# Layer 0's attention: values multiplied four items behind the scores, maps joined by one operation, negated maxima, squares of two blocks at once

## The reference, cut to what matters

```
def _diff_attend(q, k, v, lam):
    s = jnp.einsum('bqhmd,bkhmd->bhmqk', q, k).astype(jnp.float32) / math.sqrt(q.shape[-1])
    p = jax.nn.softmax(s, axis=-1)
    a = p[:, :, 0] - lam * p[:, :, 1]
    return jnp.einsum('bhqk,bkhd->bqhd', a.astype(v.dtype), v)

def out_proj(o):                       # inside _diff_mixer
    o = _rmsnorm(o, subln_g) * (1.0 - lam_init)
    return o.reshape(o.shape[0], o.shape[1], -1) @ w_o
```

## Time and profile before

| | |
|---|---|
| median of 3 runs | 3017.91 us (3016.14 to 3020.22) |
| the profiled execution | 3016.83 us, of which the span of instructions is 3015.6 us |
| TensorE busy over the span | 2670.6 us (89%) |
| vector engine busy | 751.3 us (25%) |
| scalar engine busy | 483.6 us (16%) |
| DMA | 690.23 MB, mean 229 GB/s |

### The profile page before, as it was taken

How to read it: one execution, slowest core, us unless ns; L and a number is a source line. 1 busy time by engine, 2 the same in 40 slices (tenths; PEclk the granted TensorE clock), 3 DMA queues, 4 the chain that set the end, 5 groups by cost and what they waited for, 6 DMA issues and landing times.

```text
span 3015.6 us, 57462 instructions
## 1 busy us (share of the span) xinstructions
PE 2670.6 (89%) x24534; PEld 1982.5 (66%) x24534; DVE 751.3 (25%) x2039; ACT 483.6 (16%) x1182; POOL 212.8 (7%) x392
## 2 busy tenths in 40 slices
PE   8999999999999999997998899988776998776676
PEld 7888788887888778885444456665555466544444
DVE  2002520023002430014116621211113163332323
ACT  2001310011001220003104521110002151000001
POOL 1001010011001010001000012221211000000000
PEclk9999999999999999998999999999988999999999
DMA  7553465546453455542320039999996314999997
GB/s 265 179 171 112 157 239 173 174 157 223 153 192 111 162 202 203 195 157 106 144 84 29 3 144 375 411 411 421 420 420 236 105 52 179 420 419 419 419 419 296
DMA packets 251832, 690.23 MB, mean 229 GB/s; under 512 B 15247, under 2 KB 142942, under 8 KB 235230
## 3 DMA queue, kind: packets, MB, share of 16 engines
q1 hardware_dynamic: 240352, 675.27, 59.0%
q0 software_dynamic: 7552, 10.76, 1.0%
q10 hardware_dynamic: 3710, 0.99, 0.1%
HBM read 669.95 MB, written 17.04 MB: 228 GB/s over the span
## 4 chain that ended last, share of the span: by engine, by line
PE 76%; DMA 12%; DVE 5%; issue 3%; ACT 3%; SPq 0%; ACTq 0%; POOL 0%; POOLq 0%; DVEq 0%
PE ps L663 18%; DMA arena<-in_moe_w_up 11%; PE ps L674 10%; PE ps L1443 5%; PE ps L2287 5%; PE ps L2262 3%; PE ps L2790 3%; PE ps L2302 3%; PE ps L1497 2%; PE ps L894 2%; PE ps L687 2%; PE ps L1054 2%; PE ps L2042 2%; PE ps L2751 1%; PE ps L2814 1%
## 5 line engine op out<-in xcount | busy, mean ns | idle before, releaser
L663 PE MATMUL ps<-arena 128*128 128x256 f32 x2560 | 568.6, 379 | 3.5 <-DVE arena L745 3.5
L663 PEld LDWEIGHTS ps<-arena 128*128 128x128 f32 x2560 | 483.0, 189 | 73.8 <-issue 4.1
L674 PE MATMUL ps<-arena 128*128 128x256 f32 x1408 | 318.0, 379 | 0.0
L674 PEld LDWEIGHTS ps<-arena 128*128 128x128 f32 x1408 | 264.9, 189 | 46.1 <-issue 8.4
L2287 PE MATMUL ps<-arena 128*32 128x128 f32 x6016 | 193.6, 286 | 61.1 <-issue 58.6
L2287 PEld LDWEIGHTS ps<-arena 128*32 128x32 f32 x6016 | 177.6, 115 | 71.9 <-issue 67.6
L2790 PE MATMUL ps<-arena 128*32 128x128 f32 x4096 | 138.7, 294 | 82.3 <-issue 80.6
L787 DVE TENSOR_TENSOR arena<-arena,ps 128x256 f32<-128x256 f32 x76 | 32.1, 422 | 638.4 <-ACT arena L755 633.7
L2790 PEld LDWEIGHTS ps<-arena 128*32 128x32 f32 x4096 | 125.5, 118 | 90.0 <-issue 89.0
L1443 PE MATMUL ps<-arena 128*128 128x512 f32 (+1 forms) x384 | 162.6, 601 | 5.6 <-ACT arena L1390 5.6
L755 ACT ACTIVATE arena<-ps 128x256 f32<-128x256 f32 x76 | 29.2, 384 | 675.1 <-PE ps L663 675.1
(11 more groups left out here) (457 smaller groups left out, 3091.6 us busy)
## 6 DMA issues: line engine op xcount, KB each, us to landing
arena<-in_moe_w_gate SPq DMA_DIRECT2D x64, 2048.0 KB, 24.8
arena<-in_moe_w_up SPq DMA_DIRECT2D x64, 2048.0 KB, 25.5
arena<-in_moe_w_down SPq DMA_DIRECT2D x64, 2048.0 KB, 30.4
arena<-in_mod_w SPq DMA_DIRECT2D x24, 2048.0 KB, 13.0
arena<-in_w_gate SPq DMA_DIRECT2D x44, 1024.0 KB, 5.3
arena<-in_w_up SPq DMA_DIRECT2D x44, 1024.0 KB, 7.9
arena<-in_w_down SPq DMA_DIRECT2D x44, 1024.0 KB, 4.8
arena<-in_w_in SPq DMA_DIRECT2D x12, 1024.0 KB, 6.0
```

What stands on the lines that cost most here:

```text
L663: last = pe.matmul(k.ps[:, T % 4, off:off + S], w[:, t, T % 2 * P:(T % 2 + 1) * P], h[:, t, :], start=(t == 0), stop=(t == KT - 1), skip_g ...
L674: last = pe.matmul(acc[:, t, :], d[:, T % 2, t * P:(t + 1) * P], k.hid[:, T % 4, :], start=(T == 0 and t % 2 == 0), stop=end, skip_group_c ...
```

## The change

In layer 0's attention:

- The factor 0.125 moves from the exponentials and the negation into the queries, where they are projected. For that the projection's two products become three-operand operations with a constant factor (0.125 for q0, 1 for all other tags), and the context's copy gets a scale.
- The maximum is written negated; the operation of line 1599 is gone.
- The maps are joined unnormalised by the first sum: with the row sums s0 and s1, p0 + (-lam s0 / s1) p1 is made by one operation over the map, with a one-element operation ahead of it for the factor. The operation over the whole second map (line 1607) is gone. The missing 1/s0 comes in when the output is copied out of PSUM.
- The values' matmuls, and with them the output's copy, run four items behind the scores.
- The squares are taken for two blocks at once, every second item, five items behind, without an accumulated sum; the vector engine sums them, six items behind. The root waits for the last of these sums.
- The small statistics lie in six rows of ten columns in place of four of sixteen.

Cut to its core:

```diff
+def factor_of(tag):
+    return 0.125 if tag == "q0" else 1.0
...
 def dve_project_tile(k, tag, dst, ntok, j):
-    V.tensor_tensor(dst[:, j, 0:S], k.ps[:, j % 4, 0:S], k.c["cosx"], ALU.mult).then_inc(*s["pr_cos"].up(tag, j))
+    V.scalar_tensor_tensor(dst[:, j, 0:S], k.ps[:, j % 4, 0:S], f, k.c["cosx"], ALU.mult, ALU.mult).then_inc(*s["pr_cos"].up(tag, j))
     V.wait_ge(*s["pr_rot"].at(tag, j))
-    V.tensor_tensor(tmp, k.ps[:, 4 + j % 2, 0:S], k.c["sinx"], ALU.mult).then_inc(*s["pr_sin"].up(tag, j))
+    V.scalar_tensor_tensor(tmp, k.ps[:, 4 + j % 2, 0:S], f, k.c["sinx"], ALU.mult, ALU.mult).then_inc(*s["pr_sin"].up(tag, j))
...
 def pe_attend(k, l, items):
-    N, maps = len(items), 2 if l else 1
-    for n in range(N + 3):
+    N, maps, behind = len(items), 2 if l else 1, 3 if l else 4
+    for n in range(N + behind):
...
-        i = n - 3
+        i = n - behind
...
 def dve_attend_a(k, items):
-            V.tensor_reduce(st[:, 0:2], ps[:, 2 * (n % 2):2 * (n % 2) + 2, 0:nk], AX, ALU.max).then_inc(*step.up())
-            V.wait_ge(*step.last())
-            V.tensor_scalar(st[:, 2:4], st[:, 0:2], -0.125, None, ALU.mult).then_inc(*step.up(0, n))
+            V.tensor_reduce(stats(k, n)[:, 0:2], ps[:, 2 * (n % 2):2 * (n % 2) + 2, 0:nk], AX, ALU.max, negate=True).then_inc(*step.up(0, n))
...
             V.reciprocal(st[:, 6:8], st[:, 4:6]).then_inc(*step.up())
             V.wait_ge(*step.last())
-            V.tensor_scalar(pr[:, 1, :], pr[:, 1, :], st[:, 7:8], k.lam[:, 2:3], ALU.mult, ALU.mult).then_inc(*step.up())
+            V.scalar_tensor_tensor(st[:, 8:9], st[:, 4:5], k.lam[:, 2:3], st[:, 7:8], ALU.mult, ALU.mult).then_inc(*step.up())
             V.wait_ge(*step.last())
-            V.scalar_tensor_tensor(pr[:, 0, :], pr[:, 0, :], st[:, 6:7], pr[:, 1, :], ALU.mult, ALU.add).then_inc(*s["wt_dve"].up(0, i))
-        i = n - 3
-        if i >= 0:
+            V.scalar_tensor_tensor(pr[:, 0, :], pr[:, 1, :], st[:, 8:9], pr[:, 0, :], ALU.mult, ALU.add).then_inc(*s["wt_dve"].up(0, i))
+        i = n - 4
+        if 0 <= i < N:
             q, t = items[i][0], items[i][1]
             V.wait_ge(*s["av_done"].at(0, i))
-            V.tensor_copy(rows_of(k)[:, t, q * P:(q + 1) * P], ps[:, 6 + i % 2, 0:P]).then_inc(*s["av_out_dve"].up(0, i))
+            V.tensor_scalar(rows_of(k)[:, t, q * P:(q + 1) * P], ps[:, 6 + i % 2, 0:P], stats(k, i)[:, 6:7], None, ALU.mult).then_inc(*s["av_out_dve"].up(0, i))
+        i = n - 6
+        if i >= 0 and i % 2:
+            q, t = items[i][0], items[i][1]
+            V.wait_ge(*s["av_squared"].at(0, i))
+            V.tensor_reduce(k.ss.rearrange("p (t h) -> p t h", t=4)[:, t - 1:t + 1, q:q + 1], two_blocks(k.rscale2), AX, ALU.add).then_inc(*s["av_summed"].up(0, i))
...
 def act_attend_a(k, items):
-                last = act.activation(pr[:, m, :], ps[:, 2 * (n % 2) + m, 0:nk], ACT.Exp, bias=st[:, 2 + m:3 + m], scale=0.125, accum_out=st[:, 4 + m:5 + m])
+                last = act.activation(pr[:, m, :], ps[:, 2 * (n % 2) + m, 0:nk], ACT.Exp, bias=st[:, m:1 + m], accum_out=st[:, 4 + m:5 + m])
             last.then_inc(*s["sc_exp"].up(0, n))
-        i = n - 4
-        if i >= 0:
+        i = n - 5
+        if i >= 0 and i % 2:
             q, t = items[i][0], items[i][1]
             act.wait_ge(*s["av_out_dve"].at(0, i))
-            if i > 0:
-                act.wait_ge(*s["av_squared"].at(0, i - 1))
-            act.activation(k.rscale2[:, 0:P], rows_of(k)[:, t, q * P:(q + 1) * P], ACT.Square,
-                           accum_out=k.ss[:, t * 8 + q:t * 8 + q + 1]).then_inc(*s["av_squared"].up(0, i))
+            if i >= 2:
+                act.wait_ge(*s["av_summed"].at(0, i - 2))
+            act.activation(two_blocks(k.rscale2), rows_of(k)[:, t - 1:t + 1, q * P:(q + 1) * P], ACT.Square).then_inc(*s["av_squared"].up(0, i))
...
 def act_attention_a_end(k):
-    act.wait_ge(*s["av_squared"].last())
+    act.wait_ge(*s["av_summed"].at(0, len(items_a()) - 1))
```

More of the change, by code:

```diff
@@ L1464, in act_project_tile @@
     if ntok > S:
[L1465 removed]
+        act.activation(dst[:, j, S:2 * S], k.ps[:, j % 4, S:2 * S], ACT.Copy, scale=factor_of(tag)).then_inc(*s["pr_copied"].up(tag, j, "ctx"))
 def dve_project(k, tag, dst, ntok, tiles):
@@ L1473, in dve_project_tile @@
 def dve_project_tile(k, tag, dst, ntok, j):
-    V, s = k.nc.vector, k.s
+    V, s, f = k.nc.vector, k.s, factor_of(tag)
     tmp = k.pr2[:, j % 2, 0:S]
     V.wait_ge(*(s["pr_copied"].at(tag, j, "ctx") if ntok > S else s["pr_copied"].at(tag, j)))
-    V.tensor_tensor(dst[:, j, 0:S], k.ps[:, j % 4, 0:S], k.c["cosx"], ALU.mult).then_inc(*s["pr_cos"].up(tag, j))
+    V.scalar_tensor_tensor(dst[:, j, 0:S], k.ps[:, j % 4, 0:S], f, k.c["cosx"], ALU.mult, ALU.mult).then_inc(*s["pr_cos"].up(tag, j))
     V.wait_ge(*s["pr_rot"].at(tag, j))
-    V.tensor_tensor(tmp, k.ps[:, 4 + j % 2, 0:S], k.c["sinx"], ALU.mult).then_inc(*s["pr_sin"].up(tag, j))
+    V.scalar_tensor_tensor(tmp, k.ps[:, 4 + j % 2, 0:S], f, k.c["sinx"], ALU.mult, ALU.mult).then_inc(*s["pr_sin"].up(tag, j))
     V.wait_ge(*s["pr_cos"].last())
@@ L1591, in dve_attend_a @@
     step = s["sc_dve"]
-    for n in range(N + 3):
+    for n in range(N + 6):
         if n < N:
             nk = items[n][4]
-            st = k.st[:, n % 4, :]
             V.wait_ge(*s["sc_done"].at(0, n))
-            V.tensor_reduce(st[:, 0:2], ps[:, 2 * (n % 2):2 * (n % 2) + 2, 0:nk], AX, ALU.max).then_inc(*step.up())
-            V.wait_ge(*step.last())
-            V.tensor_scalar(st[:, 2:4], st[:, 0:2], -0.125, None, ALU.mult).then_inc(*step.up(0, n))
+            V.tensor_reduce(stats(k, n)[:, 0:2], ps[:, 2 * (n % 2):2 * (n % 2) + 2, 0:nk], AX, ALU.max, negate=True).then_inc(*step.up(0, n))
         i = n - 1
@@ L1602, in dve_attend_a @@
             nk = items[i][4]
-            pr, st = probs(k, i, nk), k.st[:, i % 4, :]
+            pr, st = probs(k, i, nk), stats(k, i)
             V.wait_ge(*s["sc_exp"].at(0, i))
@@ L1606, in dve_attend_a, with stats, two_blocks @@
             V.wait_ge(*step.last())
-            V.tensor_scalar(pr[:, 1, :], pr[:, 1, :], st[:, 7:8], k.lam[:, 2:3], ALU.mult, ALU.mult).then_inc(*step.up())
+            V.scalar_tensor_tensor(st[:, 8:9], st[:, 4:5], k.lam[:, 2:3], st[:, 7:8], ALU.mult, ALU.mult).then_inc(*step.up())
             V.wait_ge(*step.last())
-            V.scalar_tensor_tensor(pr[:, 0, :], pr[:, 0, :], st[:, 6:7], pr[:, 1, :], ALU.mult, ALU.add).then_inc(*s["wt_dve"].up(0, i))
-        i = n - 3
-        if i >= 0:
+            V.scalar_tensor_tensor(pr[:, 0, :], pr[:, 1, :], st[:, 8:9], pr[:, 0, :], ALU.mult, ALU.add).then_inc(*s["wt_dve"].up(0, i))
+        i = n - 4
+        if 0 <= i < N:
             q, t = items[i][0], items[i][1]
             V.wait_ge(*s["av_done"].at(0, i))
-            V.tensor_copy(rows_of(k)[:, t, q * P:(q + 1) * P], ps[:, 6 + i % 2, 0:P]).then_inc(*s["av_out_dve"].up(0, i))
+            V.tensor_scalar(rows_of(k)[:, t, q * P:(q + 1) * P], ps[:, 6 + i % 2, 0:P], stats(k, i)[:, 6:7], None, ALU.mult).then_inc(*s["av_out_dve"].up(0, i))
[4 more added lines that the diff above has]
+            V.tensor_reduce(k.ss.rearrange("p (t h) -> p t h", t=4)[:, t - 1:t + 1, q:q + 1], two_blocks(k.rscale2), AX, ALU.add).then_inc(*s["av_summed"].up(0, i))
+def stats(k, n):
+    return k.st.rearrange("p a b -> p (a b)")[:, n % 6 * 10:n % 6 * 10 + 10]
+def two_blocks(tile):
+    return tile.rearrange("p (t d) -> p t d", t=2)
 def act_attend_a(k, items):
@@ L1619, in act_attend_a @@
     N = len(items)
-    for n in range(N + 4):
+    for n in range(N + 5):
         if n < N:
             nk = items[n][4]
-            st, pr = k.st[:, n % 4, :], probs(k, n, nk)
+            st, pr = stats(k, n), probs(k, n, nk)
             act.wait_ge(*s["sc_dve"].at(0, n))
```

2 lines of the change are left out of this document (1 added, 1 removed).

## The result

The changed kernel takes 2999.21 us in the median (2992.55 to 3001.21), the kernel before beside it 3017.86; the ratio is 0.9934, with a 95% interval of 0.9917 to 0.9951. That is 18.65 us faster, inside the range of 2990 to 3009 and 3 us above the 2996 forecast. The profiled execution took 3001.21 us (span 3000.0), 15.6 us less span than the one before.

The account below looks back on a forecast made before the run. Layer 0's attention was held half by the vector engine, half by a copy-values-transposes-scores loop. Gains of 3.0, 16.5 and 4.3 us made 23.8, less 1.8 for small delays 22.0: 2996 us, range 2990 to 3009.

Parts of the forecast that it names:

- the loop: Layer 0's attention, half of each head: copy of the turned map, values, transposes and next scores hold the pace, 5.44 us.
- The loop over three items: Layer 0's attention with later values: the copy-values-transposes-scores chain takes 5.08 us against 5.92 of vector work; TensorE next, 8.14 a head.
- The fear about 0.03 us of margin: Layer 0's attention: some scores arrive only about 0.03 us early, so small delays add 0.2 us a head, 1.8 us.
- The vector engine's head, 8.64: Layer 0's attention: vector operations of one head of four items, summed by start distances, cost 8.64 us, above TensorE's 8.14.
- the deduction: 1.8 us taken off the 23.8 us gain for small delays of scores in layer 0's attention, leaving 22.0.
- first head: Start of layer 0's attention: falls from 11.60 to 8.64 us, taken as a full head, gain 3.0 us.
- six heads: Middle of layer 0's attention: 68.32 us less six heads at 8.64, gain 16.5 us.
- last stretch: End of layer 0's attention, to the reciprocal behind the root: 18.41 us becomes 14.06, gain 4.3 us.
- The last sum is hidden under the table load: End of layer 0's attention: the root's table load starts behind the square without awaiting the sum; otherwise 0.45 us.
- The gain passes one for one: Behind layer 0's attention: the expert weight stream's start moves with the stage, so the stage's gain reaches the kernel's end.
- rival (c): Layer 0's attention: TensorE, nearly full, meets its low clock; at share 0.6 13 us slower, 3031 us; chance 0.04.
- The Trainium skill's rule: Layer 0's attention: no two vector operations overlap, so a head takes 9.6 us, 8 us more in all, 3004; chance 0.06.

Follow-up runs that it names:

- the lag alone: Kernel before with only the values' matmuls, their copy out and the squares one item later, operations unchanged: stage 86.32 us, head 10.03, median 11.5 us faster.
- the cuts alone: Changed kernel with values' matmuls back to three items behind, squares and sums one item earlier: stage 89.24 us, head 10.45.

## Why the prediction was right

- *What bounds the stage.* Right on both counts: the loop (the lag alone removes the wait) and the vector engine (the cuts alone keep the wait of 0.91). The expectation for the lag alone, 10.05 us a head out of rows 2, met 10.03.
- *The loop over three items stops binding, TensorE is next.* Right: 1.8 us of waits left in the middle stretch, and once the vector engine was relieved it was TensorE that worked throughout (34.00 of 34.00 us, at 8.48 a head). The square's new wait and the copy's wait in the same iteration cost nothing there. The fear about 0.03 us of margin, for which I took off 1.8 us (0.2 us a head would be 1.6 over eight), didn't come true: no gap in the vector engine's rows.
- *The vector engine's head, 8.64.* It measured 9.08. Two terms were too small. The one-element factor, priced by the negation's 0.17, took 0.219, and the scaled copy out, priced by the plain copy's 0.29, took 0.345. That is 0.05 and 0.06 per item, 0.11 x 4 = 0.44 a head, exactly the difference. The others of the vector engine were right: the sum 0.411 (0.43 taken), the negated maximum 1.217 against 1.222, so free. The paired square of the scalar engine was sized wrong, 0.413 for 0.32, but that engine had room. The projections' products with three operands, taken as 0.05 dearer each, cost nothing: 0.419 and 0.423 against 0.420 and 0.424.
- *The sum.* 23.8 us before the deduction, 22.0 forecast, 20.7 measured. By parts, against the forecast ahead of the deduction: first head 3.1 (3.0), six heads 14.0 (16.5), last stretch 3.6 (4.3), together 20.7. The 2.5 us of the six heads are the two prices; of the 0.7 in the last stretch 0.38 is that 7.73 us lie behind the last maximum and not 7.35, and the rest the two prices again. The first head came out near by luck: 8.52 us at a granted clock of 0.80 and without a copy out or a sum, where a full head of 8.64 was taken. And both figures for the six heads hold the 2.1 us of low clock before, which the forecast counted as gain without saying so. Of the miss of 3.1 us the deduction of 1.8 for the thin margin, which did not exist, covered more than half. That is luck: by its own reasons the forecast was 23.8.
- *The last sum is hidden under the table load.* Right. The sum on the vector engine, then square and load on the scalar engine:

```profile
1681.47 0.42 DVE L1622 TENSOR_REDUCE arena<-arena 128x2 f32<-128x256 f32 x1 [0.54 <-ACT arena L1653]
1683.10 0.35 DVE L1743 RECIPROCAL arena<-arena 128x32 f32<-128x32 f32 x1 [1.21 <-ACT arena L1733]
```

```profile
1681.02 0.42 ACT L1653 ACTIVATE arena<-arena 128x256 f32<-128x256 f32 x1 [0.98 <-DVE arena L1622]
1681.45 1.28 ACT L1733 ACT_TABLE_LOAD   x1
```

  The load starts at 1681.45, while the sum that the root waits for runs from 1681.47 on.
- *The gain passes one for one.* Right up to layer 1's first maximum (718.74 against 718.72 us, where another kernel took 722.96). Behind it 5.4 us were lost in the profiled execution. That is the step that I did not have: I had looked at TensorE's clock only inside the changed stage, as rival (c), and there it was 1.00. The forecast took the rest of the kernel as rigid, and it is not: the same code can meet another clock when it arrives at another time, by whatever rule.
- *The Trainium skill's rule.* "VectorE: DVE Perf Modes", section "The DRAIN you can't avoid", as the prediction read it, would have given 9.6 us a head, and 9.98 with the durations now measured. The changed kernel's head of 9.08 has starts 0.09 us before the end of the operation ahead (1642.21 against 1641.08 + 1.22), so the measurement decides against that reading for independent neighbours. The Trainium skill's same section goes on, "A next op that is not held starts earlier", which the prediction left out; the rows fit that sentence.

## What to carry to other kernels

When two bounds of nearly equal length alternate in a pipeline, find both before changing either: here the lag and the cuts alone took 1.01 and 0.59 us off a steady head and both together 1.96, for each alone left the other one binding. Compare heads at the same granted clock: two slow heads before would have made the parts look additive. Once one engine is full, every operation on it counts at its start-to-start distance, and work that was moved there to spare an engine with room (the sums) should go back. Price an operation with a per-partition factor, or one that reads PSUM and scales, from a row of that very form, not from its plain cousin.

## What the runs showed of the hardware

- A maximum written negated costs nothing: 1.217 us for 1024 elements, 1.222 without.
- A copy of 128 columns out of PSUM on the vector engine took 0.285 us, with a per-partition factor 0.345; a one-element operation with a per-partition factor and a tensor operand 0.219, against 0.170 for a two-element product with a constant.
- The table load of the scalar engine starts before the wait of the instruction that needs it is over (1681.45, and 1604.27 in the earlier trace rows).
- TensorE's granted clock fell to its lower level (1.2 GHz) 64.7 to 64.9 us behind layer 1's first maximum in six of twelve executions and in none of the other six, with the same work of TensorE up to there (60.28 of 64 us busy, and a wait of 1.8 us that ends at 63.4). It cost 2.5 to 5.4 us. The six arrived between 2401.8 and 2412.3 us, the others at 2393.8 to 2400.1 or 2413.9 to 2422.6; whether the arrival decides, or the grid of times on which the low stretches start, these runs can't tell.
- Two of six equal heads before took 12.09 us at a granted clock of 0.86, the other four 11.03 to 11.04 at 1.00.
- A product of 256 columns on the vector engine took as long with three operands as with two: 0.419 and 0.423 us against 0.420 and 0.424.
